# Seven block products for eight in ten feed-forward groups of a hybrid decoder layer

## What is computed

```python
h = _rmsnorm(x, norm_g[l, 2]) * (1.0 + sc2) + sh2
y = (jax.nn.silu(h @ w_gate[l]) * (h @ w_up[l])) @ w_down[l]
x = x + g2 * _rmsnorm(y, norm_g[l, 3])
```

## Time and profile before

| | us |
|---|---|
| median of 3 runs | 1813.39 |
| lowest, highest | 1808.46, 1813.92 |
| the profiled execution's own time | 1809.81 |
| its span, first to last instruction | 1808.0 |

### The profile page before, as it was taken

One profiled execution on the slowest core, in us unless ns is written; L12 is line 12 of the kernel. 1 busy time (PEld: TensorE's weight loads), 2 busy tenths in 40 slices (PEclk: granted clock), 3 DMA queues, 4 the chain that ended last, 5 costly groups with the idle time before them and its releaser, 6 DMA issues.

```text
span 1808.0 us, 22125 instructions
## 1 busy us (share of the span) xinstructions
PE 1724.1 (95%) x8276; PEld 1440.8 (80%) x8276; DVE 883.5 (49%) x1572; ACT 548.0 (30%) x920; POOL 629.1 (35%) x355
## 2 busy tenths in 40 slices
PE   2899999999999999989999999999999999999996
PEld 2787878877888888888888788888888888888885
DVE  5614746568999999375684431122122022122116
ACT  1433335373332222256324452111111210210213
POOL 0622120103445655500786233213322322421424
PEclk9999999998999999999999999999999999999998
DMA  8121141010111111501873301102101111111202
GB/s 288 76 61 56 58 111 34 15 51 30 47 40 58 44 58 41 180 13 58 299 251 99 126 13 58 47 24 70 58 30 51 58 35 46 59 45 35 70 23 93
DMA packets 35142, 131.43 MB, mean 73 GB/s; under 512 B 4368, under 2 KB 4368, under 8 KB 35088
## 3 DMA queue, kind: packets, MB, share of 16 engines
q1 hardware_dynamic: 32848, 123.36, 20.3%
q0 software_dynamic: 2240, 7.34, 1.9%
HBM read 114.43 MB, written 9.96 MB: 69 GB/s over the span
## 4 chain that ended last, share of the span: by engine, by line
PE 91%; DVE 4%; DMA 2%; ACT 1%; issue 1%; SPq 0%; POOL 0%; DVEq 0%; ACTq 0%
PE ps L493 27%; PE ps L494 27%; PE ps L495 27%; PE ps L692 4%; PE ps L671 2%; PE ps L597 1%; DMA region_b<-in_w_ada 1%; PE ps L598 1%; DVE region_a L1765 1%; PE ps L523 1%; DMA raw<-in_w_ffn 1%; PE ps L515 0%; PE ps L703 0%; DVE region_a L1779 0%; DVE region_c L1427 0%
## 5 line engine op out<-in xcount | busy, mean ns | idle before, releaser
L493 PE MATMUL ps<-h_t,w_t 128*128 128x512 f32 x1472 | 577.1, 392 | 2.3 <-DVE y_t L1628 1.3
L495 PE MATMUL ps<-h_t,w_t 128*128 128x512 f32 x1472 | 574.3, 390 | 0.0
L494 PE MATMUL ps<-h_t,w_t 128*128 128x512 f32 x1472 | 574.2, 390 | 0.0
L493 PEld LDWEIGHTS ps<-h_t,w_t 128*128 128x128 f32 x1472 | 277.4, 188 | 61.5 <-issue 4.2
L494 PEld LDWEIGHTS ps<-h_t,w_t 128*128 128x128 f32 x1472 | 277.5, 189 | 57.6 <-issue 0.7
L495 PEld LDWEIGHTS ps<-h_t,w_t 128*128 128x128 f32 x1472 | 277.2, 188 | 57.9
L1774 DVE TENSOR_TENSOR region_d<-ps,region_d 128x512 f32<-128x512 f32 x40 | 27.7, 692 | 407.6 <-PE ps L495 407.6
L1243 POOL TENSOR_TENSOR w_t<-raw,w_t 128x1280 fp32r<-128x1280 f32 (+1 forms) x50 | 142.6, 2852 | 205.6 <-ACT w_t L918 115.5
L1520 DVE MAX8 top<-region_b 128x8 f32<-128x384 f32 (+5 forms) x192 | 157.9, 882 | 17.3 <-issue 16.7
L1523 DVE MATCH_REPLACE8 region_b<-top,region_b 128x384 f32<-128x384 f32 (+5 forms) x192 | 166.1, 876 | 0.0
L1779 DVE TENSOR_TENSOR region_a<-ps,region_a 128x512 f32<-128x512 f32 x160 | 110.0, 691 | 98.8 <-PE ps L495 98.8
(11 more groups left out here) (208 smaller groups left out, 2386.7 us busy)
## 6 DMA issues: line engine op xcount, KB each, us to landing
raw<-in_w_ffn SPq DMA_DIRECT2D x66, 512.0 KB, 3.6
region_b<-in_w_ada SPq DMA_DIRECT2D x48, 512.0 KB, 4.5
raw<-in_w_gates SPq DMA_DIRECT2D x32, 640.0 KB, 3.8
raw<-in_w_z SPq DMA_DIRECT2D x18, 512.0 KB, 3.4
region_a<-in_x SPq DMA_DIRECT2D x8, 512.0 KB, 12.0
mix_dram<-region_a SPq DMA_DIRECT2D x8, 512.0 KB, 6.0
region_a<-mix_dram SPq DMA_DIRECT2D x8, 512.0 KB, 6.5
raw<-in_w_o SPq DMA_DIRECT2D x8, 512.0 KB, 3.8
```

The source lines that it names most:

```text
L493: pe.matmul(o, a_hi, m_hi, start=first, stop=False)
L494: pe.matmul(o, a_hi, m_lo, start=False, stop=False)
L495: return pe.matmul(o, a_lo, m_hi, start=False, stop=last)
```

## The change

In groups 1 to 10 the two gate tiles together, and the two up tiles together, are a 2 x 2 block product: rows are the two tiles f, the inner dimension is split in k-blocks 0 to 3 and 4 to 7, columns are the two token halves. One level of Strassen's algorithm (Winograd's form) makes it of seven block products (`step`: four k-blocks of three matmuls) in place of eight, first for gate (g = 0), then for up (g = 1).

- The four sums of blocks of h (t1 to t4) are made once, during group 0, on DVE and POOL, and split by ACT, DVE and POOL. t1 and t2 take the place of x1, which is written to DRAM and read back in the last group; t3 replaces a block of h; t4 lies in y_t.
- The sums of weight blocks are made by POOL in every group (`combine`, five for each g, 128x512 each).
- 14 weight operands of 128x512 and four halves of the down weights (18 a group) pass through six slots, split by ACT (`slot_split`) and POOL (`slot_rest`). There are three raw buffers (the third is region_d).
- A step waits for its operand, and where it takes or adds to a PSUM bank, for what was read from that bank. ACT (`first_term`) and DVE (`sums`) put the results together in SBUF; silu runs there but for one quarter; DVE multiplies (`product`) and makes the activation's low part (`a_rest`), which POOL did before.
- The down product starts when three of the four activation quarters are split. It runs by column halves c (by t in the last group) and uses banks 0 to 3.

The core of the diff (empty lines are left out):

```diff
-FFN_AT = (0, 1, 3, 5)
-FFN_AHEAD = ((1,), (2, 3), (4, 5), (6,))
+PIECES = (0, 3, 1, 5, 2, 4)
+SLOTS = 6
+OPERANDS, STEPS = 18, 14
+STEP_BANK = (0, 1, 2, 1, 3, 0, 3)
+STEP_NEW = (True, True, True, False, True, False, False)
...
+        w_flat = w_t[:, :, :, :].rearrange("p a b n -> p (a b n)")
+        slot_of = [w_flat[:, n * L:(n + 1) * L] for n in range(SLOTS - 1)] + [slot_c[:, :]]
...
+        raw_at = [raw[:, 0, 0:D], raw[:, 1, 0:D], region_d[:, :]]
...
+        t1, t2 = (wide_b[:, 0], wide_b[:, 1]), (wide_b[:, 2], wide_b[:, 3])
...
+        step_moving = (b11, t2, t4, t3, t1, b21, b22)
...
+        LATE = ((1, 0), (1, 1), (0, 0), (0, 1))
+        PAIR = ((0, 1), (2, 0))
+        def operand(n):
+            if n >= 14:
+                return raw_at[1 + (n - 14) % 2][:, (n - 14) // 2 * HALF:(n - 14) // 2 * HALF + HALF]
+            g, s = n // 7, n % 7
+            a, b = PAIR[g]
+            if s == 1:
+                return slot_f[n % SLOTS]
+            src = raw_at[b if s in (2, 4) else a]
+            return src[:, HALF:L] if s in (2, 5, 6) else src[:, 0:HALF]
...
+                if j == 4:
+                    for t in range(TT):
+                        sp.wait_ge(s_x1, t + 1)
+                        sp.dma_start(x1_dram[:, t, :], x1[:, t]).then_inc(s_x1_out, 16)
                 tile_load(T_FFN + j, w_ffn[m])
...
+            def piece_load(i, p, ahead=0):
+                m = PIECES[p] + 6 * ahead
+                sp.dma_start(raw_at[p % 3], w_ffn[i * 6 + m]).then_inc(s_piece[p % 3], 16)
...
+            def group_pieces(i, last):
...
+                sp.wait_ge(s_slot_lo, made(i, 6))
+                piece_load(i, 3)
+                piece_load(i, 4)
+                sp.wait_ge(s_slot_lo, made(i, 13))
+                piece_load(i, 5)
+                if last:
+                    return
+                piece_load(i, 0, 1)
+                sp.wait_ge(s_slot_lo, made(i, 16))
+                piece_load(i, 1, 1)
+                sp.wait_ge(s_slot_lo, made(i, 17))
+                piece_load(i, 2, 1)
...
+            for j, step in ((1, 9), (0, 12)):
+                sp.wait_ge(s_step, count(FG - 1, STEPS, step))
+                for t in range(4 * j, 4 * j + 4):
+                    sp.dma_start(x1[:, t], x1_dram[:, t, :]).then_inc(s_x1_in[j], 16)
...
+            def first_down():
                 for q in range(2 * TT):
-                    t, c = q // 2, q % 2
+                    c, t = q // TT, q % TT
...
+                    if q >= 4:
+                        pe.wait_ge(s_yf, q - 3)
+                    down_product(4 + q % 4, t, c)
...
+            def step(i, g, s):
...
+                pe.wait_ge(s_slot_lo, made(i, n))
+                if g == 0 and STEP_NEW[s]:
+                    pe.wait_ge(s_yf, count(i, 2 * TT, 2 * TT + STEP_BANK[s] - 3))
+                if s == 3:
+                    pe.wait_ge(s_u, count(i, 10, 5 * g + 1))
+                if s == 5:
+                    pe.wait_ge(s_first, count(i, 2, g + 1))
+                if s == 6:
+                    pe.wait_ge(s_u, count(i, 10, 5 * g + 4))
+                if s in (1, 2, 3, 4):
+                    T = (2, 4, 3, 1)[s - 1]
+                    pe.wait_ge(s_t_lo[T], 2 if T == 3 else 1)
...
+                for k in range(KT // 2):
+                    w = slice(k * P, (k + 1) * P)
+                    mm = product(ps[:, 4 * g + STEP_BANK[s], :], hi[:, w], lo[:, w], m_hi[:, k], m_lo[:, k],
+                                 new and k == 0, k == KT // 2 - 1, not new)
+                mm.then_inc(s_step, 1)
...
+                for g in range(2):
+                    for s in range(7):
+                        step(i, g, s)
+                for q in range(2 * TT):
+                    c, t = (q % 2, q // 2) if last else (q // TT, q % TT)
                     if q == 0:
-                        pe.wait_ge(s_a_lo, 2 if first else i * 4 + 3)
-                    if q == TT:
-                        pe.wait_ge(s_a_lo, 4 if first else i * 4 + 4)
-                    if not first:
+                        pe.wait_ge(s_act_lo, count(i, 4, 3))
+                    if t == TT // 2:
+                        pe.wait_ge(s_act_lo, count(i, 4, 4))
+                    if (q < 2 if last else t == 0):
+                        pe.wait_ge(s_slot_lo, made(i, 15 + 2 * c))
+                    if q >= 4:
                         pe.wait_ge(s_yf, i * 16 + (q - 3))
-                    elif q >= 4:
-                        pe.wait_ge(s_yf, q - 3)
-                    for f in range(2):
-                        tok = slice(t * P, (t + 1) * P)
-                        cc = slice(c * HALF, (c + 1) * HALF)
-                        mm = product(ps[:, 4 + q % 4, :], y_t[:, 0, 0, f, tok], y_t[:, 0, 1, f, tok],
-                                     y_t[:, 1, 0, f, cc], y_t[:, 1, 1, f, cc], f == 0, f == 1)
-                    mm.then_inc(s_y, 1)
+                    down_product(q % 4, t, c)
...
+                    act.wait_ge(s_step, count(i, STEPS, n - SLOTS + 1, ahead))
...
+                act.activation(slot_hi[n % SLOTS], operand(n), ACT.Copy).then_inc(s_slot_hi, 1)
...
+            def silu(i, v):
...
+                if (f, half) == (0, 0):
+                    act.wait_ge(s_step, count(i, STEPS, 6))
+                    act.activation(at, ps[:, 0, :], ACT.Silu).then_inc(s_silu3, 1)
+                else:
+                    act.wait_ge(s_u, count(i, 10, {0: 3, 1: 4, 3: 5}[v]))
+                    act.activation(at, at, ACT.Silu).then_inc(s_silu3, 1)
...
+            def a_hi(i, v):
+                act.wait_ge(s_act, count(i, 4, v + 1))
+                act.activation(quarter(y_hi(0), *LATE[v]), quarter(act_lo, *LATE[v]), ACT.Copy).then_inc(s_act_hi, 1)
...
+                first_term(i, 0)
+                for n in (6, 7, 8, 9):
+                    slot_split(i, n)
+                silu(i, 0)
+                slot_split(i, 10)
+                silu(i, 1)
+                silu(i, 2)
+                slot_split(i, 11)
+                slot_split(i, 12)
+                silu(i, 3)
+                first_term(i, 1)
+                for n in (13, 14, 15, 16):
+                    slot_split(i, n)
+                a_hi(i, 0)
+                slot_split(i, 17)
+                a_hi(i, 1)
+                if not last:
+                    slot_split(i, 0, 1)
+                a_hi(i, 2)
+                a_hi(i, 3)
+                if not last:
+                    for n in range(1, SLOTS):
+                        slot_split(i, n, 1)
...
+            for n in range(14, 18):
+                first_down_split(n)
+            t_hi(2, s_t2_sum)
+            first_silu(3)
+            t_hi(1, s_t1_sum)
+            first_a_hi(3)
+            t_hi(4, s_t4_sum)
+            slot_split(1, 0)
+            t_hi(3, s_t3_sum[0], slice(0, 2))
+            slot_split(1, 1)
+            t_hi(3, s_t3_sum[1], slice(2, 4))
+            for n in range(2, SLOTS):
+                slot_split(1, n)
...
+            def slot_rest(i, n, ahead=0):
...
+                pool.tensor_tensor(slot_lo[n % SLOTS], operand(n), slot_hi[n % SLOTS].bitcast(F32),
+                                   ALU.subtract).then_inc(s_slot_lo, 1)
...
+            def combine(i, g, k, ahead=0):
...
+                if k == 1:
+                    pool.wait_ge(s_slot_lo, made(i, n0, ahead))
+                    pool.wait_ge(s_piece[PAIR[g][1]], count(i, 32, 32 if g else 16, ahead))
+                    ins = pool.tensor_tensor(a[:, low], a[:, low], b[:, low], ALU.subtract)
+                elif k == 2:
+                    slot_free(i, n0 + 1, ahead)
+                    pool.wait_ge(s_combined, count(i, 10, 5 * g + 1, ahead))
+                    ins = pool.tensor_tensor(slot_f[(n0 + 1) % SLOTS], b[:, high], a[:, low], ALU.subtract)
+                elif k == 3:
+                    pool.wait_ge(s_combined, count(i, 10, 5 * g + 1, ahead))
+                    ins = pool.tensor_tensor(b[:, low], b[:, low], b[:, high], ALU.add)
+                elif k == 4:
+                    pool.wait_ge(s_slot_lo, made(i, n0 + 5, ahead))
+                    ins = pool.tensor_tensor(a[:, high], a[:, high], b[:, high], ALU.subtract)
+                else:
+                    pool.wait_ge(s_combined, count(i, 10, 5 * g + 4, ahead))
+                    ins = pool.tensor_tensor(a[:, high], a[:, high], a[:, low], ALU.add)
+                ins.then_inc(s_combined, 1)
+            def next_operands(i, ahead, upto=SLOTS):
...
+                slot_rest(i, 0, ahead)
+                for k in (1, 2, 3):
+                    combine(i, 0, k, ahead)
+                for n in range(1, SLOTS):
+                    slot_rest(i, n, ahead)
+                for k in (4, 5):
+                    combine(i, 0, k, ahead)
+            def ffn_group(i, last):
+                slot_rest(i, 6)
+                slot_rest(i, 7)
+                for k in (1, 2, 3):
+                    combine(i, 1, k)
+                for n in range(8, 13):
```

(104 more changed lines are left out.)

290 lines of the change are left out of this document (194 added, 96 removed).

## The result

| | before | after |
|---|---|---|
| median of 4 runs, us | 1812.45 | 1793.12 |
| lowest, highest | 1808.46, 1813.92 | 1790.29, 1795.24 |
| profiled execution: time, span | 1809.81, 1808.0 | 1790.29, 1788.5 |

The ratio is 0.9899, 95% interval 0.9885 to 0.9912: 19.3 us faster on the medians. 1788 was forecast, with a range of 1764 to 1801.

The account below looks back on a forecast made before the run. PE alone was taken to bound groups 1 to 10. Terms: -54.4 + 21 (nine joins) + 0.2 + 7 (group 0) + 1 (clock) = -25 us on 1809.8, giving 1784.6, or 1788 on the median; range 1764 to 1801.

Parts of the forecast that it names:

- 240 matmuls fewer: Groups 1 to 10: 24 matmuls fewer a group at an unchanged 0.2267 us each, 5.44 us a group, -54.4 us.
- nine joins, pauses: Between a group's two halves, before the down product: PE waits 2.3 us for the third a_rest in nine groups, +21 us.
- last group's join: Before the last group's down product: no next operands exist, so PE waits only 0.2 us.
- group 0, pause: Fifth down unit of group 0: PE waits 6.5 us for DVE's first eviction, between 0 and 11.
- group 0, later calls: Later t_rest calls in group 0 cost another 0.5 us.
- clock in group 0: Group 0's pause may lower PE's clock: between 0 and 3 us more, 1 taken.
- clock behind the joins: After the 2.3 us join waits in groups 1 to 9: no lowered clock, 0 us.
- Cover inside the steps: Within the 14 steps of a group: operands come five us or more early, so their waits cost nothing.
- the list: Turns at a join after step 12: three a_rest alternate with two POOL operations, from 0.6 to 4.8 us; PE resumes at 4.9.
- a rival for all groups at once: Joins: piece 1 lands 0.5 us later, a_rest(2) goes before combination 1, PE waits 1.2 us; 1778 us, chance 27%.
- Tail: End of the kernel, set by DVE's evictions and normalisation: order stays, cost 0, at most 1 us.
- the 2.3 us waits cost nothing more: Joins of nine groups: PE's waits cost their length alone; around an earlier 3.2 us wait the clock stayed 1.00.

Follow-up runs that it names:

- the hold: The changed kernel plus one POOL wait: the next group's operands begin only once the third activation quarter is split; 1770.36 us, ratio 0.9766.
- the late piece: The changed kernel with the next group's piece 1 loaded behind POOL's low part 17 instead of 16; 1780.72 us, ratio 0.9827.
- The runs with copies: The hold plus one, two or three DVE copies of a PSUM bank pair onto itself before the third a_rest; 1783.76, 1807.23, 1829.66 us.
- the one with two copies: The hold plus two DVE copies of a PSUM bank pair onto itself before the third a_rest; 1807.23 us, ratio 0.9967.
- the first order of group 0: The changed kernel, t3 sums behind DVE's fourth eviction, t4 and t3 low parts later, POOL's last activation low part before t1's; 1788.76 us, ratio 0.9871.

## Why the prediction was right, and its one wrong step

| term, us | forecast | in the trace after |
|---|---|---|
| 240 matmuls fewer | -54.4 | -54.4 |
| nine joins, pauses | +21 | +17.1 |
| their restarts | 0 | +0.9 |
| last group's join | +0.2 | +0.7 |
| group 0, pause | +6.5 | +6.5 |
| group 0, later calls | +0.5 | 0 |
| clock in group 0 | +1 | +2.5 |
| clock behind the joins | 0 | +4.8 |
| sum | -25 | -21.9 |
| measured, by the spans | | -19.5 |

("Restarts" are the second matmul behind a pause, which starts 0.33 us after the first in place of 0.227.) The terms were missed in both directions: the nine joins were put 3.9 us too dear, the clock 6.3 us too cheap. That the whole is only 5.7 us off on the profiled executions (1784.6 forecast, 1790.3 measured) is in part luck.

- **Matmuls and their pitch: right.** Shapes stayed, and with the hold PE is busy 539.88 of 540 us at a granted clock of 1.00.
- **Cover inside the steps: right for groups 2 to 10.** In group 1 it was there only because PE had stood in group 0 before: once that pause went, operands were 2.9 and 0.6 us late.
- **The join: the mechanism and its times were right.** Three a_rest in 4.1 us for the 4.2 of the list, PE back 4.9 us behind step 12. The hold shows the cause, the late piece shows the order of the requests. The size was too large by 4 us, because in four of nine groups less than the full list of turns came true: piece 1 landed too late for combination 1 to go ahead of a_rest(2). The forecast had it 0.5 us early, the rows show 0.4 us early to 0.3 late. I had given this as a rival for all groups at once; it was a mixture.
- **Group 0: right in place and size**, and by the turns: DVE's sum took 5.58 us beside a low part of 5.54. The forecast allowed 0 to 11 us for this pause, so that it met 6.5 exactly is luck.
- **Tail: right.** From the start of the last matmul to the end of the span there are 15.1 us in both traces (1792.87 to 1808.0, 1773.41 to 1788.5).
- **The clock: wrong.** The step that failed is "the 2.3 us waits cost nothing more". I drew it from the 3.2 us wait of the earlier trace rows, a single case, and the rows below this list show that it was not even a typical one. Behind three of five pauses of 2.3 us the granted clock fell to the lower of its two levels, 1.2 GHz for 2.4, and eight matmuls started 0.427 us apart in place of 0.227: 1.6 us each time, 4.8 in all. Behind group 0's pause it was 12 matmuls, 2.5 us for the 1 that I took. Together the term was 7.3 us for 1, and it more than offset the joins' being shorter. The runs with copies show that it is the pause: same kernel, same place, and the slow matmuls come with its length.

**What belongs to no term, and what the single case was worth.** In the mixing stage, which the change does not touch, the wait of 3.2 us of the earlier trace rows is there again in the kernel after, and this time the clock is 0.50 around it:

```profile
PE ps L637 <- DVE diag L1732: 3.2, 1, 3.2
...
1015.00:1020.00 5.00, 4.50 (x19) 4.30 (x20) 3.67 (x10) 3.40 (x8) 0.00 (x0) 0.50 0.53 213
```

With it group 0's first product on DVE came 1.85 us later than before (1091.85 for 1090.00). In the same five microseconds the kernel with the hold shows 0.72, the one with two copies 0.50, the late piece and the first order of group 0 both 1.00. It belongs to the execution, not to the change, and with it the sum comes to -20.0 for the -19.5 measured. Over the twelve traces this wait lasts 2.9 to 3.9 us, and the clock fell in it or just behind it in nine; the kernel before is one of the three in which it did not. One wait in one trace could not carry the rule that was drawn from it.

The Trainium skill ("SBUF — State Buffer", who interferes with whom) has one shared port pair for DVE and GpSimd and an exclusive lock on it. The trace agrees: three a_rest took 1.89 us with POOL held, 3.06 with one turn of POOL's between them, 4.12 with two.

## What to carry to other kernels

Before giving DVE an operation with both inputs in SBUF, look at what POOL does at that moment; if POOL has slack later, one wait that holds it until DVE's short chain is through is worth more than a rebalancing of the work (here 23 us for one line; moving the low parts back to POOL gained nothing). Price a wait of PE not by its length alone: from about 2 us on, add the matmuls that follow at the lower clock, and in a loop expect it in a part of the iterations. When an order is changed to remove a wait, look for the same wait in the stage behind it.
